# Feed-forward in two passes over its weights, half of its tokens normed inside the second, and modulation chunks moved into local attention

## The chip, the cores and the metric

One core of one Trainium2 chip runs the whole program. The metric is the device time of one execution in microseconds. A core has PE (TensorE: matmuls and transposes, results in PSUM), DVE (VectorE), ACT (ScalarE), POOL (GpSimd) and SP, whose queue issues most of the loads. Each engine works through its own list of instructions in order and waits on semaphores for the others.

## The reference

Two layers over 1024 latent tokens and 256 context tokens, 1024 wide, in fp32. Each layer mixes tokens with three kinds of attention and then runs a feed-forward part. A modulation (six vectors of 1024 per stream and layer, from one product with `w_ada`) shifts, scales and gates.

```python
m_lat = jnp.split((silu_c @ w_ada[layer] + b_ada[layer])[:, None, :], 6, axis=-1)
...
y_lat = jnp.concatenate([gla_lat, diff_lat, swa_lat], axis=-1) @ w_out[layer]
h_lat_mid = post_norm(h_lat, y_lat, m_lat[2], ln_g[layer, 0], ln_b[layer, 0])
h_lat_next = swiglu_sublayer(h_lat_mid, m_lat[3], m_lat[4], m_lat[5], w_ffn_gate[layer],
                             w_ffn_up[layer], w_ffn_down[layer], ln_g[layer, 1], ln_b[layer, 1])

def modulate(x, shift, scale):
    return (_ln_plain(x) * (1.0 + scale.astype(F32)) + shift.astype(F32)).astype(x.dtype)

def post_norm(h, y, gate, g, b):
    return layer_norm(DN_ALPHA * h + gate * y, g, b)

def swiglu_sublayer(h, shift, scale, gate, w_g, w_u, w_d, g, b):
    u = modulate(h, shift, scale)
    f = (jax.nn.silu(u @ w_g) * (u @ w_u)) @ w_d
    return post_norm(h, f, gate, g, b)
```

The context stream does the same in layer 0 with its own modulation; in layer 1 only the latent tokens go through the feed-forward. The hidden width is 2816 = 22 tiles of 128.

## The kernel before

The program is a row of stages, one after the other, each with its own buffers: modulation (the first six chunks), input norm, input projection, gated linear attention, differential attention, local (sliding window) attention, attention norm (output projection included), feed-forward, feed-forward norm; then layer 1 from its input projection on. Every stage ends with all engines done.

fp32 products are made of three matmuls: each operand is split into a high part and the rest (`hi`, `lo`), and `product` (L122 to L127) issues hi*hi, hi*lo, lo*hi.

**Feed-forward (`swiglu`, from L1965).** The 22 hidden tiles are taken as 11 groups of two. A group has six weight blocks of 128x1024 (512 KB), j = 0 to 5: gate and up of the first hidden tile, gate and up of the second, and the two down blocks. SP loads a block into `raw` (three buffers), ACT copies the high part (L2032), POOL subtracts to get the low part (L2061). The tokens are taken in `CHUNKS`: 512 and 512 latent tokens and 256 context tokens in layer 0, the first two in layer 1. For each of the two hidden tiles PE makes gate, then up, for all chunks; ACT takes silu of gate (L2040), DVE multiplies it with up (L2125), POOL splits the product into `hhi` and `hlo` (L2067, L2069). Then PE makes the down product per token tile and half, into `ffn_acc`, and DVE adds it to `Y` in SBUF (L2130), which POOL has set to zero at the start (L2057). PE waits before a tile's down product for the hidden part of the tile's chunk:

```python
                pe.wait_ge(w_ready, g * 6 + 6)
                for n, tt in enumerate(order):
                    pe.wait_ge(hid_ready, g * 2 * NC + NC + chunk_of[tt] + 1)
```

Groups 1 to 9 are a hardware loop, groups 0 and 10 are written out. ACT may overwrite a high part once its last reader is done (`release`).

**Norm of tiles (`norm_tiles`, from L216).** One function for three kinds (input, attention, ffn). Per tile of 128 tokens, for kind ffn: SP loads the residual `h_mid`; DVE multiplies `Y` by the gate (L447), adds the residual (L450), takes statistics (L424, L426); ACT takes the root (L495), DVE the reciprocal and the negated mean (L432, L434), ACT normalizes (L499), POOL multiplies by `ln_g` (L543), DVE adds `ln_b` (L456) and SP stores. In layer 0 a second normalization follows, for the next layer's input: statistics, root, normalize into `x`, eight transposes on PE (L406), eight modulating instructions on ACT (L511), high part on DVE (L469), low part on POOL (L548). The steps of neighbouring tiles are staggered by hand. In layer 0 this stage also makes eight chunks of 512 of layer 1's modulation: 2 MB of `w_ada` per chunk (L342), a product (L398), the bias (L478).

**Local attention (`sliding_window_attention`, from L1370).** Per tile of 128 queries and per key group: scores on PE, shift and maximum on DVE (L1604), exponential on ACT (L1542), scaling on POOL (L1465), transposes (L1504), product with V (L1516). The order is written out by a list of slots. SP loads keys, then the queries of two tiles, then each further tile's queries when the scores of the tile two before are made (L1453).

## Time and profile before

| | us |
|---|---|
| median of 3 runs (4255.87 to 4266.93) | 4262.75 |
| profiled execution, its own time | 4264.5 |
| its span, first to last instruction | 4262.2 |
| PE busy (of the span) | 3553.8 (83%) |
| DVE, ACT, POOL busy | 1611.0, 1299.4, 1434.5 |
| mean granted clock of PE | 0.91 |

A busy PE is one with a matmul under way; matmuls overlap, so the distance between starts is what one costs in a stream. The span is a row of stages with all engines handed over between them, so a stage can be read by itself. The granted clock is 1.00 at 2.4 GHz and 0.50 at 1.2 GHz; means over a stretch lie between.

### The profile page before, as it was taken

Reading aid. Unit: us, or ns where it says so; the run is one execution under the profiler, and the core shown is the slowest. Engines: PE = TensorE matmul, PEld = TensorE weight load, DVE = VectorE, ACT = ScalarE, POOL = GpSimd, SP = SyncE. Lnnn points to the kernel's source line nnn. Section 1 sums busy time; section 2 is a strip of 40 time slices with the busy share of each in tenths; the row PEclk is TensorE's granted clock in tenths of the full one; section 3 lists DMA queues with packets and bytes.
Section 4 is the critical chain, followed back from the end, with each engine's and each line's share of the span. In section 5 each row is a group of like instructions: output and inputs, shape, how many; then the busy total and the mean of one; then the engine's idle time right before and its main releaser. Section 6 shows DMA issues by size and latency. Waiting matters only on the chain. (4 is left out here: it accounts for less than half of the span.)

```text
span 4262.2 us, 52025 instructions
## 1 busy us (share of the span) xinstructions
PE 3553.8 (83%) x19550; PEld 2828.6 (66%) x19550; DVE 1611.0 (38%) x2555; ACT 1299.4 (30%) x2242; POOL 1434.5 (34%) x951
## 2 busy tenths in 40 slices
PE   6799596878686999999995599596966969999991
PEld 2488386555475888888881387385654758888881
DVE  2104553756472221121126404555845621222215
ACT  2211274765442011101103311375844321111111
POOL 1211242763344223323322311244923433333331
PEclk8899697788898999999997799698988979999996
DMA  8423312113331111111105323312033311111112
GB/s 287 151 86 116 100 26 64 30 37 84 102 105 58 40 40 39 34 34 44 39 15 202 132 90 111 95 31 71 15 88 90 99 59 50 49 49 49 43 36 93
DMA packets 151200, 318.19 MB, mean 75 GB/s; under 512 B 12105, under 2 KB 72489, under 8 KB 151057
## 3 DMA queue, kind: packets, MB, share of 16 engines
q1 hardware_dynamic: 128304, 260.20, 19.6%
q10 hardware_dynamic: 19072, 44.60, 2.8%
q0 software_dynamic: 3680, 11.47, 1.0%
q8 instruction: 91, 1.49, 0.1%
q14 instruction: 53, 0.43, 0.0%
HBM read 250.20 MB, written 66.03 MB: 74 GB/s over the span
## 5 line engine op out<-in xcount | busy, mean ns | idle before, releaser
L2061 POOL TENSOR_TENSOR ffn_wlo<-ffn_raw,ffn_whi 128x1024 fp32r<-128x1024 f32 x132 | 314.6, 2390 | 800.3 <-ACT ffn_whi L2032 800.3
L2125 DVE TENSOR_TENSOR ffn_hid<-ffn_up,ffn_silu 128x512 f32<-128x512 f32 (+1 forms) x110 | 70.2, 638 | 1049.0 <-PE ffn_up L127 1022.9
L2032 ACT CAST ffn_whi<-ffn_raw 128x1024 fp32r<-128x1024 f32 x132 | 136.4, 1048 | 945.1 <-PE ffn_acc L127 467.4
L2130 DVE TENSOR_TENSOR y<-ffn_acc,y 128x512 f32<-128x512 f32 x396 | 273.8, 691 | 266.8 <-PE ffn_acc L127 266.8
L125 PE MATMUL ffn_gate<-second_uhi,ffn_whi 128*128 128x512 f32 (+1 forms) x880 | 325.9, 370 | 37.3 <-POOL ffn_wlo L2061 37.3
L126 PE MATMUL ffn_gate<-second_ulo,ffn_whi 128*128 128x512 f32 (+1 forms) x880 | 325.3, 370 | 0.0
L127 PE MATMUL ffn_gate<-second_uhi,ffn_wlo 128*128 128x512 f32 (+1 forms) x880 | 325.1, 369 | 0.0
L126 PE MATMUL ffn_up<-second_ulo,ffn_whi 128*128 128x512 f32 (+1 forms) x880 | 323.9, 368 | 0.0
L125 PE MATMUL ffn_up<-second_uhi,ffn_whi 128*128 128x512 f32 (+1 forms) x880 | 323.8, 368 | 0.0
L127 PE MATMUL ffn_up<-second_uhi,ffn_wlo 128*128 128x512 f32 (+1 forms) x880 | 323.7, 368 | 0.0
L125 PE MATMUL ffn_acc<-ffn_whi,ffn_hhi 128*128 128x512 f32 x792 | 308.2, 389 | 0.0
L126 PE MATMUL ffn_acc<-ffn_wlo,ffn_hhi 128*128 128x512 f32 x792 | 308.2, 389 | 0.0
L127 PE MATMUL ffn_acc<-ffn_whi,ffn_hlo 128*128 128x512 f32 x792 | 308.1, 389 | 0.0
L637 POOL TENSOR_TENSOR in_wlo<-in_raw,in_whi 128x1024 fp32r<-128x1024 f32 x42 | 100.2, 2387 | 453.3 <-ACT in_whi L661 453.3
L1920 DVE TENSOR_SCALAR_CACHE_REDUCE diff_scores<-diff_scores 128x1280 f32<-128x1280 f32 (+1 forms) x144 | 196.7, 1383 | 66.5 <-PE diff_scores L1774 65.2
L125 PEld LDWEIGHTS ffn_gate<-second_uhi,ffn_whi 128*128 128x128 f32 x880 | 167.0, 190 | 66.3 <-POOL ffn_wlo L2061 38.1
L1844 ACT ACTIVATE diff_e<-diff_scores,diff_negmax 128x1280 f32<-128x1280 f32 (+1 forms) x144 | 178.2, 1238 | 66.8 <-DVE diff_scores L1920 65.8
L2040 ACT ACTIVATE ffn_silu<-ffn_gate 128x512 f32<-128x512 f32 (+1 forms) x110 | 61.1, 556 | 448.5 <-PE ffn_gate L127 448.5
L125 PE MATMUL in_acc<-first_uhi,in_whi 128*128 128x512 f32 (+1 forms) x504 | 179.5, 356 | 20.7 <-POOL in_wlo L637 20.7
L1898 POOL TENSOR_TENSOR diff_w<-diff_w,diff_e 128x1280 f32<-128x1280 f32 (+1 forms) x72 | 191.9, 2666 | 6.0
L126 PEld LDWEIGHTS ffn_gate<-second_ulo,ffn_whi 128*128 128x128 f32 x880 | 167.0, 190 | 28.2
L127 PEld LDWEIGHTS ffn_gate<-second_uhi,ffn_wlo 128*128 128x128 f32 x880 | 166.8, 190 | 28.0
(270 smaller groups left out, 8157.8 us busy)
## 6 DMA issues: line engine op xcount, KB each, us to landing
ffn_raw<-w_ffn_dram SPq DMA_DIRECT2D x132, 512.0 KB, 3.6
in_raw<-w_in_dram SPq DMA_DIRECT2D x42, 512.0 KB, 3.5
norm_input_ada_w<-w_ada_dram SPq DMA_DIRECT2D x10, 2048.0 KB, 9.2
norm_ffn_ada_w<-w_ada_dram SPq DMA_DIRECT2D x8, 2048.0 KB, 8.0
proj_scratch<-in_stage ACTq DMA_DIRECT2D x20, 640.0 KB, 2.9
ada_w<-w_ada_dram SPq DMA_DIRECT2D x6, 2048.0 KB
gla_kq<-proj_scratch SPq DMA_DIRECT2D x32, 320.0 KB
swa_qhl<-heads_scratch SPq DMA_DIRECT2D x36, 256.0 KB
```

Source lines behind the costliest of these rows:

```text
L125: pe.matmul(out, st_hi, mv_hi, start=start, stop=False)
L126: pe.matmul(out, st_hi, mv_lo, start=False, stop=False)
L127: return pe.matmul(out, st_lo, mv_hi, start=False, stop=stop)
L637: pool.tensor_tensor(wlo[:, s, :, :], raw[:, s, :].rearrange("p (k n) -> p k n", k=KT), whi[:, s, :, :].bitcast(F32), ALU.subtract).then_i ...
L1844: act.activation(E[:, r % 4, c, 0:keys], SC[:, c, 0:keys], ACT.Exp, bias=ng[:, c:c + 1], scale=-1.0, accum_out=den[:, c, tile_of(i, r), r ...
L1898: pool.tensor_tensor(w, w, E[:, u % 4, 0, 0:keys], ALU.add).then_inc(w_done, 1)
L1920: dve.tensor_scalar(SC[:, c, 0:keys], SC[:, c, 0:keys], -scale, 3e38, ALU.mult, ALU.min, accum_out=ng[:, c:c + 1]).then_inc(neg_done, 1)
L2032: act.copy(whi[:, j % 3, :], raw[:, j % 3, :]).then_inc(w_hi, 1)
L2040: act.activation(sg[:, c, 0:tn], GT[:, c, 0:tn], ACT.Silu).then_inc(silu_done, 1)
L2061: pool.tensor_tensor(wlo[:, j % 3, :], raw[:, j % 3, :], whi[:, j % 3, :].bitcast(F32), ALU.subtract).then_inc(w_ready, 1)
L2125: dve.tensor_tensor(hf[:, c, 0:tn], UP[:, c, 0:tn], sg[:, c, 0:tn], ALU.mult).then_inc(mul_done, 1)
L2130: dve.tensor_tensor(Y[:, tt, cols], ACC[:, half, :], Y[:, tt, cols], ALU.add).then_inc(y_added, 1)
```

## The change

Three parts.

1. `swiglu` goes over the weights twice. Pass 0 takes the first 512 latent tokens and, in layer 0, the 256 context tokens; pass 1 the other 512 latent tokens. All is written out, with no hardware loop. `raw`, and the banks of gate and up, have two buffers instead of three; silu's result is multiplied in place. The first group of a pass copies into `Y`, so nothing is set to zero.
2. In pass 1 the tiles of pass 0 are normed, one tile in each of the groups 1, 2, 4, 5, 7, 8 (layer 0) or 1, 2, 4, 5 (layer 1), with all the steps of the ffn norm, in layer 0 the transposes and the modulation too. `norm_tiles` for kind ffn is left with the last four tiles.
3. The ffn norm of layer 0 makes no modulation chunks. Local attention of layer 1 makes them, one per query tile.

```diff
-        chunked = modulated and not attn
+        chunked = kind == "input"
@@ sliding_window_attention
+            chunks = [(1, c) for c in range(4, ADA_CHUNKS)]
+            shares = [1] * len(tiles)
...
+                if b == 1:
+                    for n in range(min(AR, len(chunks))):
+                        load_chunk(n)
+                if b >= 2:
+                    for n in chunks_at(b - 2):
+                        if n + AR < len(chunks):
+                            load_chunk(n + AR)
...
+            def modulation_chunk(b, n):
+                pe.wait_ge(w_in[n % AR], 80 * (n // AR + 1))
...
+                for kt in range(KT):
+                    for j in range(4):
+                        mm = pe.matmul(O[32 * j:32 * j + 32, b % 2, k * P:(k + 1) * P], cs[:, kt, :], W[:, n % AR, kt, j * P:(j + 1) * P],
+                                       start=(kt == 0), stop=(kt == KT - 1))
+                mm.then_inc(product_done, 1)
@@ swiglu
+        passes = [CHUNKS[0:1] if last else [CHUNKS[0], CHUNKS[2]], [CHUNKS[1]]]
+        group_of = [1 + 3 * k // 2 for k in range(NT)]
...  SP
+            for p in range(2):
+                for g in range(G):
+                    if p == 0 and g == 1:
+                        load_residual(0)
+                    for j in range(6):
+                        load_weight(p, g, j)
+                        if j == 3 and p == 1 and g - 1 in group_of:
+                            k = group_of.index(g - 1)
+                            store(k)
+                            if k + 1 < NT:
+                                load_residual(k + 1)
...  ACT
+                    if k is not None:
+                        normalize(k, 0, Y[:, normed_tiles[k], :])
+                    silu(p, g, 0)
+                    split(p, g, 3)
+                    split(p, g, 4)
+                    silu(p, g, 1)
+                    split(p, g, 5)
+                    if k is not None and not last:
+                        if k == 0:
+                            act.wait_ge(one_plus, 1)
+                        normalize(k, 1, x[:, :])
+                        modulate(k)
+                    if following(p, g)[0] < 2:
+                        for j in range(3):
+                            split(*following(p, g), j)
...  PE
+                    pe.wait_ge(w_ready, weight(p, g, 5) + 1)
+                    for n, (c, tt, at) in enumerate(tiles_of(p)):
+                        pe.wait_ge(hid_ready, unit(p, g, 1, c) + 1)
+                        if n == 2 and norm_tile(p, g) is not None and not last:
+                            turn(norm_tile(p, g))
...  DVE
+                    if not last and norm_tile(p, g - 1) is not None:
+                        high_part(norm_tile(p, g - 1))
+                    if k is not None:
+                        residual(k)
+                    multiply(p, g, 0)
+                    if k is not None:
+                        shifted(k)
+                    multiply(p, g, 1)
@@ build
-                    swiglu(nc, t, res, layer, LAT_CHUNKS if last else CHUNKS)
-                    norm_tiles(nc, t, res, "ffn", layer, tiles, last)
+                    swiglu(nc, t, res, layer, last)
+                    norm_tiles(nc, t, res, "ffn", layer, everything[(N_CTX + BANK) // P:], last)
```

`residual(k)` on DVE is the product with the gate, the wait for the residual load, the sum and the statistics up to the negated mean; `shifted(k)` is the addition of `ln_b` and, in layer 0, the second statistics.

The lists of instructions show it at three places. POOL in the feed-forward of layer 0, first a group before (`wlo` low part of a weight, `hhi` and `hlo` parts of a chunk's hidden values):

```order
L2061 TENSOR_TENSOR ffn_wlo<-ffn_raw,ffn_whi 128x1024 x4
L2067 CAST ffn_hhi<-ffn_hid 128x512
L2069 TENSOR_TENSOR ffn_hlo<-ffn_hid,ffn_hhi 128x512
L2067 CAST ffn_hhi<-ffn_hid 128x512
L2069 TENSOR_TENSOR ffn_hlo<-ffn_hid,ffn_hhi 128x512
L2067 CAST ffn_hhi<-ffn_hid 128x256
L2069 TENSOR_TENSOR ffn_hlo<-ffn_hid,ffn_hhi 128x256
L2061 TENSOR_TENSOR ffn_wlo<-ffn_raw,ffn_whi 128x1024 x2
```

and now, group 2 of pass 1, with the low part of the tile of group 1 (`second_ulo`) and the scaling of its own (`y<-y,ffn_lng`):

```order
L2239 TENSOR_TENSOR ffn_wlo<-ffn_raw,ffn_whi 128x1024 x4
L2258 TENSOR_TENSOR second_ulo<-ffn_x,second_uhi 128x8x128
L2253 TENSOR_TENSOR y<-y,ffn_lng 128x1024
L2245 CAST ffn_hhi<-ffn_silu 128x512
L2247 TENSOR_TENSOR ffn_hlo<-ffn_silu,ffn_hhi 128x512
L2239 TENSOR_TENSOR ffn_wlo<-ffn_raw,ffn_whi 128x1024 x2
L2245 CAST ffn_hhi<-ffn_silu 128x512
L2247 TENSOR_TENSOR ffn_hlo<-ffn_silu,ffn_hhi 128x512
L2239 TENSOR_TENSOR ffn_wlo<-ffn_raw,ffn_whi 128x1024 x4
```

One chunk instead of three per hidden tile stands between the weights, and two instructions of the norms come behind weight 3, ahead of the hidden parts.

ACT in the same stage, before:

```order
L2032 CAST ffn_whi<-ffn_raw 128x1024 x3
L2040 ACT_TABLE_LOAD
L2040 ACTIVATE ffn_silu<-ffn_gate 128x512 x2
L2040 ACTIVATE ffn_silu<-ffn_gate 128x256
L2032 CAST ffn_whi<-ffn_raw 128x1024 x2
L2040 ACTIVATE ffn_silu<-ffn_gate 128x512 x2
L2040 ACTIVATE ffn_silu<-ffn_gate 128x256
L2032 CAST ffn_whi<-ffn_raw 128x1024 x4
```

and in group 1 of pass 1:

```order
L2191 ACT_TABLE_LOAD
L2191 ACTIVATE ffn_sd<-ffn_mv,ffn_eps 128x1
L2195 ACTIVATE y<-y,ffn_nmu,ffn_rstd 128x1024
L2187 ACT_TABLE_LOAD
L2187 ACTIVATE ffn_silu<-ffn_gate 128x512
L2179 CAST ffn_whi<-ffn_raw 128x1024 x2
L2187 ACTIVATE ffn_silu<-ffn_gate 128x512
L2179 CAST ffn_whi<-ffn_raw 128x1024
L2191 ACT_TABLE_LOAD
L2191 ACTIVATE ffn_sd<-ffn_mv,ffn_eps 128x1
L2195 ACTIVATE ffn_x<-y,ffn_nmu,ffn_rstd 128x1024
```

The root and the normalization of the tile (L2191, L2195) now stand ahead of the first silu, with a table load on either side.

SP in local attention of layer 1, before (`khh` and `kll` keys, `qhl` queries):

```order
L1447 DMA swa_khh<-heads_scratch 64x2x1408
L1448 DMA swa_kll<-heads_scratch 64x2x1408
L1447 DMA swa_khh<-heads_scratch 64x2x1408
L1448 DMA swa_kll<-heads_scratch 64x2x1408
L1453 DMA swa_qhl<-heads_scratch 64x8x128 x16
```

and now, from the queries of the first two tiles on:

```order
L1486 DMA swa_qhl<-heads_scratch 64x8x128 x4
L1476 DMA swa_ada_w<-w_ada_dram 128x8x512
L1479 DMA swa_ada_b<-b_ada_dram 2x128 x4
L1476 DMA swa_ada_w<-w_ada_dram 128x8x512
L1479 DMA swa_ada_b<-b_ada_dram 2x128 x4
L1476 DMA swa_ada_w<-w_ada_dram 128x8x512
L1479 DMA swa_ada_b<-b_ada_dram 2x128 x4
L1476 DMA swa_ada_w<-w_ada_dram 128x8x512
L1479 DMA swa_ada_b<-b_ada_dram 2x128 x4
L1486 DMA swa_qhl<-heads_scratch 64x8x128 x2
L1476 DMA swa_ada_w<-w_ada_dram 128x8x512
```

Four loads of `w_ada` (2 MB each) now lie between the queries of the second tile and those of the third.

## Rows read from the trace of the kernel before

**Rows 1.** Busy time by stage: feed-forward and norm of layer 0, then of layer 1.

```profile
core 0: us, PE busy (x) PEld busy (x) DVE busy (x) ACT busy (x) POOL busy (x), PEclk, DMA share, GB/s
1327.60:2247.40 919.80, 907.36 (x4488) 771.91 (x4488) 191.86 (x286) 101.96 (x133) 273.40 (x199) 0.99 0.12 38
2247.40:2405.90 158.50, 78.46 (x208) 22.37 (x208) 112.27 (x149) 60.69 (x121) 53.52 (x29) 0.77 0.53 186
3441.50:4175.00 733.50, 721.02 (x3168) 596.43 (x3168) 152.09 (x220) 93.52 (x111) 248.43 (x156) 0.99 0.15 47
4175.00:4262.20 87.20, 0.00 (x0) 0.00 (x0) 48.51 (x64) 13.56 (x17) 20.43 (x12) 0.52 0.33 114
```


**Rows 2.** Timeline, a group of layer 1: start us, us, engine, line; PE, DVE, POOL.

```profile
3759.67 0.39 PE L127 MATMUL ffn_up<-second_uhi,ffn_wlo 128*128 128x512 f32 x1
3759.90 0.39 PE L125 MATMUL ffn_acc<-ffn_whi,ffn_hhi 128*128 128x512 f32 x1
...
3760.16 0.69 DVE L2125 TENSOR_TENSOR ffn_hid<-ffn_up,ffn_silu 128x512 f32<-128x512 f32 x1 [4.75 <-PE ffn_up L127]
...
3761.01 0.61 POOL L2067 CAST ffn_hhi<-ffn_hid 128x512 fp32r<-128x512 f32 x1 [3.47 <-DVE ffn_hid L2125]
3761.71 1.29 POOL L2069 TENSOR_TENSOR ffn_hlo<-ffn_hid,ffn_hhi 128x512 fp32r<-128x512 f32 x1
```


**Rows 3.** Timeline of DVE: residual products of both feed-forward norms.

```profile
2265.93 1.22 DVE L447 TENSOR_TENSOR norm_ffn_h<-y,norm_ffn_gate 128x1024 f32<-128x1024 f32 x1
...
2296.95 1.23 DVE L447 TENSOR_TENSOR norm_ffn_h<-y,norm_ffn_gate 128x1024 f32<-128x1024 f32 x1 [1.38 <-ACT norm_ffn_x L499]
...
2372.49 1.98 DVE L447 TENSOR_TENSOR norm_ffn_h<-y,norm_ffn_gate 128x1024 f32<-128x1024 f32 x1 [0.75 <-ACT norm_ffn_x L499]
...
4184.34 1.22 DVE L447 TENSOR_TENSOR norm_ffn_h<-y,norm_ffn_gate 128x1024 f32<-128x1024 f32 x1 [10.12 <-DMA norm_ffn_lnb<-ln_b_dram]
...
4210.59 1.82 DVE L447 TENSOR_TENSOR norm_ffn_h<-y,norm_ffn_gate 128x1024 f32<-128x1024 f32 x1 [2.95 <-DMA out_dram<-norm_ffn_h]
...
4246.92 2.21 DVE L447 TENSOR_TENSOR norm_ffn_h<-y,norm_ffn_gate 128x1024 f32<-128x1024 f32 x1 [2.56 <-DMA out_dram<-norm_ffn_h]
```


**Rows 4.** Timeline, start of the feed-forward stage of layer 0: ACT, POOL.

```profile
1331.20 1.04 ACT L2032 CAST ffn_whi<-ffn_raw 128x1024 fp32r<-128x1024 f32 x1 [8.48 <-DMA ffn_raw<-w_ffn_dram]
...
1327.57 8.63 POOL L2057 MEMSET y<- 128x10240 f32 x1 [1.70 <-POOLq L213]
1336.16 7.00 POOL L2061 TENSOR_TENSOR ffn_wlo<-ffn_raw,ffn_whi 128x1024 fp32r<-128x1024 f32 x3
```


**Rows 5.** Timeline of PE in the attention norm, and the windows behind it.

```profile
1211.29 0.50 PE L125 MATMUL norm_attention_y<-norm_attention_wohi,norm_attention_mhi 128*128 128x512 f32 x1 [2.26 <-POOL norm_attention_mlo L539]
...
1212.10:1215.50 3.40, 3.40 (x10) 2.66 (x9) 3.19 (x8) 0.41 (x2) 0.00 (x0) 0.51 0.00 0
1215.50:1218.90 3.40, 3.40 (x16) 2.83 (x15) 3.26 (x4) 1.42 (x2) 2.19 (x1) 0.99 0.87 252
```


**Rows 6.** Timeline, steps of a norm: ACT in layer 1, DVE and ACT in layer 0.

```profile
4188.58 1.28 ACT L495 ACT_TABLE_LOAD   x1 [46.15 <-DVE norm_ffn_mv L426]
...
4190.60 1.24 ACT L499 ACTIVATE norm_ffn_h<-norm_ffn_h,norm_ffn_nmu,norm_ffn_rstd 128x1024 f32<-128x1024 f32 x1 [0.43 <-DVE norm_ffn_nmu L434]
...
2293.24 2.33 DVE L434 SCALAR_TENSOR_TENSOR norm_ffn_nmu<-norm_ffn_mv,norm_ffn_rstd 128x1 f32<-128x1 f32 x1
...
1319.83 2.90 ACT L511 ACTIVATE norm_attention_x<-norm_attention_tr,norm_attention_shift,norm_attention_scale 128x128 f32<-128x128 f32 x8 [2.06 <-PE norm_attention_tr L406]
```


**Rows 7.** DMA issues: tokens loaded in the norm (KB each, us to landing).

```profile
norm_ffn_hres<-h_mid_scratch SPq DMA_DIRECT2D x18, 512.0 KB, 4.4
```


**Rows 8.** Local attention of layer 1; a chunk in the first stage; a modulation load.

```profile
3244.00:3264.00 20.00, 19.10 (x113) 11.31 (x110) 12.59 (x32) 10.72 (x27) 7.77 (x10) 1.00 0.06 14
...
28.47 3.20 PE L184 MATMUL ada_acc<-ada_w,silu_c 128*2 128x128 f32 x64 [2.12 <-DMA ada_b<-b_ada_dram]
...
norm_ffn_ada_w<-w_ada_dram SPq DMA_DIRECT2D x8, 2048.0 KB, 8.0
```

More of the change, by code:

```diff
@@ L1414, in sliding_window_attention, with chunks_at, chunk_of @@
         heads = t["heads"]
+        if layer == 0:
+            chunks, shares = [], [0] * len(tiles)
+        else:
+            chunks = [(1, c) for c in range(4, ADA_CHUNKS)]
+            shares = [1] * len(tiles)
+        def chunks_at(b):
+            first = sum(shares[:b])
+            return range(first, first + shares[b])
+        def chunk_of(m, c):
+            b, k = m // 2, c // 2
+            return sum(shares[:b]) + k if m % 2 == 0 and 0 <= m < NG and k < shares[b] else None
         def by_act(x):
@@ L1522, in _ @@
                     score(n, j)
+                if c % 2 == 0 and chunk_of(m, c) is not None:
+                    modulation_chunk(m // 2, chunk_of(m, c))
                 if c < turns_of(m):
@@ L1583, in _ @@
                     store((n - LAG - 1) // 2)
+                _, _, m, c = slots[max(s - 2, 0)]
+                if s >= 2 and c % 2 == 0 and chunk_of(m, c) is not None:
+                    store_chunk(chunk_of(m, c))
+            for s in range(AR):
+                act.wait_ge(row_out[s], 64 * len(chunks[s::AR]))
             for s in range(2):
@@ new lines, in swiglu, with stream, columns, tiles_of @@
+        block = ctx.enter_context(nc.Block())
+        const_loads = 16 * ((0 if last else 4) + 2)
+        def stream(k):
+            return 0 if normed_tiles[k] < CTX_TILES else 1
+        def columns(p, c):
+            first = sum(tn for _, tn in passes[p][:c])
+            return slice(first, first + passes[p][c][1])
+        def tiles_of(p):
+            return [(c, t0 // P + a, columns(p, c).start + a * P) for c, (t0, tn) in enumerate(passes[p]) for a in range(tn // P)]
+        def unit(p, g, f, c):
+            return sum(2 * G * len(passes[q]) for q in range(p)) + (2 * g + f) * len(passes[p]) + c
@@ new lines, in last_unit, with y_count, y_group, weight @@
+        def last_unit(p, g, f):
+            return unit(p, g, f, len(passes[p]) - 1)
+        def y_count(p, g, n, half):
+            return sum(2 * G * len(tiles_of(q)) for q in range(p)) + 2 * (g * len(tiles_of(p)) + n) + half + 1
+        def y_group(p, g):
+            return y_count(p, g, len(tiles_of(p)) - 1, 1)
+        def weight(p, g, j):
+            return (p * G + g) * 6 + j
+        def following(p, g):
+            return (p, g + 1) if g + 1 < G else (p + 1, 0)
+        def norm_tile(p, g):
+            return group_of.index(g) if p == 1 and g in group_of else None
@@ new lines, in load_residual, with store @@
+            def load_residual(k):
+                if k:
+                    sp.wait_ge(summed, k)
+                tt = normed_tiles[k]
+                if k == 0 or stream(k) != stream(k - 1):
+                    sp.dma_start(gate[:, :], t["mod"][layer, 1 - stream(k):2 - stream(k), 5 * D:6 * D].to_broadcast([P, D])).then_inc(gate_in, 16)
+                sp.dma_start(hres[:, :], t["h_mid"][tt * P:(tt + 1) * P, :]).then_inc(h_in, 16)
+            def store(k):
+                tt = normed_tiles[k]
+                sp.wait_ge(h_done, k + 1)
+                rows = t["out"][(tt - CTX_TILES) * P:(tt - CTX_TILES + 1) * P, :] if last else t["h_next"][tt * P:(tt + 1) * P, :]
+                sp.dma_start(rows, Y[:, tt, :]).then_inc(h_out, 16)
@@ new lines, in residual @@
+            def residual(k):
+                y = Y[:, normed_tiles[k], :]
+                dve.wait_ge(gate_in, 16 * len({stream(i) for i in range(k + 1)}))
+                dve.wait_ge(y_added, y_group(0, G - 1))
+                dve.tensor_tensor(y, y, gate[:, :], ALU.mult).then_inc(gated, 1)
+                dve.wait_ge(gated, k + 1)
+                dve.wait_ge(h_in, 16 * (k + 1))
+                dve.scalar_tensor_tensor(y, hres[:, :], ALPHA, y, ALU.mult, ALU.add).then_inc(summed, 1)
+                dve.wait_ge(summed, k + 1)
+                statistics(k, 0)
```

368 lines of the change are left out of this document (243 added, 125 removed).

## Prediction

> **What bounds the kernel now.** I read the stage table first, then the pieces of single stages. The feed-forward stages take 919.8 and 733.5 us, 39% of the span, and PE is busy in 907.4 and 721.0 of them at a granted clock of 0.99 [rows 1]: they are PE's stream of matmuls and nothing else. One 512-column matmul follows the other every 0.227 us (3759.67 to 3759.90) [rows 2]. The norms behind them are the opposite: 158.5 us with 78.5 of PE and 87.2 us with none [rows 1], chains from one small instruction to the next. The change takes tiles out of those chains and puts them beside the matmuls, and pays with a second pass over the weights. So the question is what the matmul stream loses.
>
> **Norm stages.** Ten tiles become four in layer 0, eight become four in layer 1. Layer 0: the first residual product starts at 2265.93, the fourth at 2296.95, the tenth at 2372.49 [rows 3]. With four tiles the last one starts 31.0 us behind the first instead of 106.6, so 75.5 us go. The stage's head was 18.5 us (2247.4 to 2265.9) with a 2 MB modulation load ahead of it; layer 1's head without one was 9.3 (4175.0 to 4184.3) [rows 1, 3]. The new head has two loads of constants more than that, so I take 11.5 and a gain of 7. Layer 1: the fourth product (4210.59) starts 26.25 us behind the first, the eighth 62.6. 36.3 us go [rows 3]. Together **-118.8 us**. The first feed-forward matmul no longer waits for the 8.63 us memset of y: with the casts at 1331.20 + 1.04 the first low part could run from 1332.3 instead of 1336.16 [rows 4]; 3.8 us in each layer, **-7.6**. The six constant loads now issued there by POOL fit before 1332.
>
> **The bare second pass.** Matmuls keep their number: every chunk of tokens still meets every weight once. The weight preparation doubles, 132 more splits on POOL, three of which took 7.00 us [rows 4]. A group of the second pass has 96 gate and up matmuls and 48 of the down product, 144 x 0.227 = 32.7 us; POOL needs 6 x 2.33 + 2 x 1.98 = 18.0 of it (3761.01 to 3763.0 is a hidden part [rows 2]), the loads 6 x 0.5 MB. Capacity is there, at no cost. The order is the trouble. The down product of a group needs the hidden part of its last chunk of tokens. Now PE runs up of chunk 0, then up of the next chunk, which hides the way of chunk 0 through DVE (product), POOL (high part) and POOL (low part). With one chunk alone nothing stands between. The way is measured in the group shown: PE stops issuing up at 3759.90, the DVE product starts at 3760.16, the low part ends at 3761.71 + 1.29 = 3763.0, and PE would go on at 3763.1 [rows 2]. That is 3.2 us without a matmul, in 11 groups of layer 0 and 22 of layer 1 (there the first pass too has one chunk): 33 x 3.2 = **+105.6**. In layer 0's first pass the 256-column chunk (24 matmuls at about 0.125, 3.0 us) hides all but 0.2: **+2**. Bounds: 2.9 to 3.5 per group.
>
> **The clock.** A pause has a second price. At 1211.29 PE resumed after 2.26 us of idle; from 1212.1 to 1215.5 the granted clock is 0.51 (the level of 1.2 GHz), and then 0.99 again (2.4 GHz); ten matmuls went in 3.4 us where the next stretch has sixteen [rows 5]. Lost: 6 matmuls, 1.4 us, up to 1.7 where the half-rate stretch is full. Not every pause of that size did it, but most did. The new pause is longer, 2.95 us by the modelled ends. I take 1.6 us in three of four pauses: 33 x 1.2 = **+40**; bounds 0 and 56.
>
> **The normed tiles.** Six tiles in layer 0 (groups 1, 2, 4, 5, 7, 8 of pass 2), four in layer 1 (1, 2, 4, 5). All times from the group's first gate matmul; up of the second half is wanted at 16.3, the down product can start at 25.0. *First tile of a pair:* from the first product to the end of the normalize it takes 4184.34 to 4191.84, 7.5 us, the table load among it [rows 3, 6]. It starts at 0.95 and is held about 2.4 by POOL's two weight splits (a one-column DVE instruction, 0.16 elsewhere, took 2.33 beside a POOL one [rows 6]): 10.9. Another table load (1.28) and silu (0.6) on ACT: 12.8. Only then comes ACT's split of weight 3 and POOL's, 16.3: just in time. Behind it POOL has the scaling 2.4, hidden 1.9, two splits 4.8: 25.4; DVE, in the second statistics until then, gives its product at 26.4, the hidden part is there at 28.5. +3.5. Then 8 transposes, 2.0 (ACT waits 2.06 for them in the row), and ACT prepares the next group's first weight only after the 2.90 us modulation [rows 6], 1.3 late: 6.6. *Second tile of a pair:* its residual load is issued only behind this group's fourth weight and the store of the tile before, at about 4.8; 512 KB take 4.4 [rows 7] and have two such in front, so it lands near 10.6. DVE stands in front of that wait with its product behind it, ACT behind DVE: weight 3 is ready at 21.1 (PE idle 4.8), and along the same chain the hidden part at 35.3, 10.3 late; with transposes and the late weight 13.5. Layer 0: 3 x 6.6 + 3 x 13.5 = 60. Layer 1 has no second statistics, no transposes: 2.4 and 8.5, 2 x 2.4 + 2 x 8.5 = 22. Sum **+82**; bounds: 12 (the transposes alone) and 110.
> The Trainium skill, GPSIMD Engine Reference, section Specifications, says that POOL shares its SBUF interface with those DVE instructions that have two SBUF inputs; the row of 2.33 us agrees. Without such holding the first tile of a pair would cost some 2.4 us less.
>
> **Modulation chunks in local attention of layer 1.** Eight chunks. PE is busy 19.1 of 20 us there [rows 8], so its added work is exposed: a chunk of 64 matmul halves took 3.20 us in the first stage (2.8 to 3.6) [rows 8]; 8 x 3.2 = 25.6. DVE's row and POOL's zeroing are hidden (vT is loaded 12 us before the first score). ACT issues 32 stores; I add 4: **+30**. What could be late is the query load of the third tile: it now stands in SP's queue behind four 2 MB loads of 8.0 us [rows 8]. They start when the first queries are in, near 3140, and end near 3170; the tile is wanted at about 3172. Nothing taken, up to 29 us if wrong. Low end 15, high end 59. In layer 0 the chunk list is empty.
>
> **Sum.** The profiled execution took 4264.5 us (span 4262.2). -118.8 - 7.6 + 105.6 + 2 + 40 + 82 + 30 = +133; 4397.7. That execution is 1.75 above the median of the three runs (4262.75), so I say **4396 us**.
>
> **Rivals.**
> 1. *Everything but the matmul stream's own pause is absorbed* (ends on the other side, faster): the normed tiles fit in the idle of DVE, ACT and POOL, the clock stays, local attention takes the chunks in its gaps. Then -118.8 - 7.6 + 107.6 = -18.8: 4244. It decides if all costs of the second pass and of the chunks stay under 126.4 / 33 = 3.8 us per single-chunk group; the pause alone is 3.2. For it: 18 of 33 us busy on POOL. Against: the in-order queues above, and PE at 19.1 of 20 in local attention. 5%.
> 2. *The clock stays at its full level*, the rest as forecast: 4356. For it: the matmuls around the pause are dense. Against: the fall at 1212 behind a shorter pause. 25%. The Trainium skill, TensorE: Matmul & The Clock Gate, section "Why this matters for your kernels", advises against pauses only where they are about this long or longer, which would give this result; [rows 5] speak against it.
> 3. *The normed tiles cost only their transposes* (a load that comes sooner, no holding): 4396 - 70 = 4326. 12%.
> 4. *The queries wait behind the modulation weights* in SP's queue: +29, 4425. 13%.
> 5. My forecast, 45%.
>
> **How the numbers follow.** 0.3% (13 us) is about what a measurement of this kernel can tell from no change. Not slower needs rival 1 or rivals 2 and 3 at once with cheap chunks (4396 - 40 - 70 - 15 = 4271): together 7%, of which 3% is faster and 4% within 0.3%. Slower by more: 93%. The range goes from rival 3 to the forecast with the upper clock bound and dearer tiles (4396 + 16 + 28): 4325 to 4440; it holds rivals 2, 3 and 4 and leaves out 1.
>
> **What would show it.** In each single-chunk group PE idle of about 3 us in front of the down product, released by POOL's low part; the group 36 us instead of 32.7 and up to 50 in groups 2, 5 and 8; half-clock stretches of 3.4 us behind the pauses and a mean clock of the second passes near 0.95; silu late behind DVE's wait for the residual load in groups 2, 5, 8; norm stages near 76 and 51 us; local attention near 194. Wrong if PE has no idle before the down product, if the clock is 1.00 through the passes, or if groups with and without a normed tile are equally long.

## The result and the profile after

The changed kernel takes 4382.8 us in the median of 4 runs (4373.4 to 4385.5), the kernel before 4259.3 in 4 runs beside it (4254.8 to 4266.9). The ratio is 1.0285, 95% interval 1.0265 to 1.0304: 2.9% slower. The forecast was 4396, between 4325 and 4440. The profiled execution of the change took 4385.5 us (span 4383.7).

Busy time by stage, in the order of [rows 1] with local attention of layer 1 in the middle (columns as there):

```profile
1327.10:2348.20 1021.10, 946.67 (x4536) 794.45 (x4536) 261.62 (x371) 227.00 (x289) 463.87 (x284) 0.96 0.24 77
2348.20:2423.10 74.90, 7.87 (x32) 6.27 (x32) 42.76 (x57) 24.83 (x49) 23.07 (x14) 0.50 0.24 77
3130.20:3316.80 186.60, 146.46 (x1259) 99.11 (x1259) 93.78 (x233) 81.69 (x188) 52.93 (x70) 0.90 0.53 150
3480.00:4335.20 855.20, 766.65 (x3168) 622.77 (x3168) 179.12 (x252) 177.34 (x193) 413.08 (x227) 0.94 0.27 88
4335.20:4383.70 48.50, 0.00 (x0) 0.00 (x0) 23.36 (x32) 7.42 (x9) 11.94 (x8) 0.53 0.32 119
```

Against the kernel before: feed-forward of layer 0 +101.3 us, its norm -83.6, local attention of layer 1 +23.0, feed-forward of layer 1 +121.7, its norm -38.7. That is +123.7; all other stages together are 2 us shorter, and the span grew by 121.5. In layer 1 PE has the same 3168 matmuls as before, yet 45.6 us more of busy time (766.7 against 721.0) and 76 us more without any. Both are losses: most of the added busy time is matmuls that take longer where the granted clock is lower (0.94 in the mean against 0.99).

A group is called single-chunk when its pass has one chunk of 512 tokens, and bare when no tile is normed in it as well. One bare group of layer 1 (3565.4 to 3602.8) from the timeline, around the end of its last up product (start, us, engine, line, operation; in brackets the idle before and who ended it). Compare [rows 2], where the matmul at 3759.90 follows the last up matmul at once:

```profile
3586.97 0.39 PE L127 MATMUL ffn_up<-second_uhi,ffn_wlo 128*128 128x512 f32 x1
...
3587.47 0.69 DVE L2360 TENSOR_TENSOR ffn_silu<-ffn_up,ffn_silu 128x512 f32<-128x512 f32 x1 [10.19 <-PE ffn_up L127]
3588.23 0.61 POOL L2245 CAST ffn_hhi<-ffn_silu 128x512 fp32r<-128x512 f32 x1 [2.26 <-DVE ffn_silu L2360]
3588.92 1.26 POOL L2247 TENSOR_TENSOR ffn_hlo<-ffn_silu,ffn_hhi 128x512 fp32r<-128x512 f32 x1
...
3590.28 0.47 PE L125 MATMUL ffn_acc<-ffn_whi,ffn_hhi 128*128 128x512 f32 x1 [2.92 <-issue]
...
3591.54 0.63 PE L126 MATMUL ffn_acc<-ffn_wlo,ffn_hhi 128*128 128x512 f32 x1
```

PE stops, DVE multiplies, POOL makes the high and the low part, which ends at 3588.92 + 1.26 = 3590.18, and 0.1 us later PE goes on. Then the matmuls take 0.63 us instead of 0.39. The windows of that group, of the two stretches behind its pause, and of the one bare group that kept its clock:

```profile
3565.40:3602.80 37.40, 34.48 (x145) 28.06 (x145) 6.91 (x10) 7.28 (x8) 17.98 (x10) 0.95 0.26 85
...
3590.90:3594.30 3.40, 3.40 (x10) 2.62 (x9) 0.69 (x1) 0.00 (x0) 1.61 (x1) 0.51 0.17 39
3594.30:3597.70 3.40, 3.40 (x16) 2.78 (x16) 1.44 (x3) 0.00 (x0) 0.00 (x0) 0.99 0.28 116
3864.90:3900.70 35.80, 32.88 (x145) 26.92 (x145) 6.92 (x10) 7.28 (x8) 18.02 (x10) 1.00 0.29 88
```

Of the 33 single-chunk groups 23 are bare. 20 of these take 37.4 to 37.6 us and have a 3.4 us stretch at 1.2 GHz behind the pause, ten matmuls where sixteen fit; one has none and takes 35.8. The two left (38.9 us, behind a group with a normed tile, and 39.0, the first of layer 1) have a mean clock of 0.91 and 0.92 and more time at the half clock. So a pause of 2.9 us costs 1.6 us more by the clock.

The ten groups with a normed tile are longer. The second one of layer 1 (3977.8 to 4023.4, 45.6 us), DVE, ACT, PE and SP:

```profile
3978.62 1.22 DVE L2334 TENSOR_TENSOR y<-y,ffn_mod_gate 128x1024 f32<-128x1024 f32 x1
3989.03 1.23 DVE L2337 SCALAR_TENSOR_TENSOR y<-ffn_hres,y 128x1024 f32<-128x1024 f32 x1 [9.20 <-DMA ffn_hres<-h_mid_scratch]
...
3991.86 0.30 ACT L2191 ACTIVATE ffn_sd<-ffn_mv,ffn_eps 128x1 f32<-128x1 f32 x1 [10.54 <-DVE ffn_mv L2324]
3992.58 1.25 ACT L2195 ACTIVATE y<-y,ffn_nmu,ffn_rstd 128x1024 f32<-128x1024 f32 x1 [0.43 <-DVE ffn_nmu L2328]
3993.85 1.28 ACT L2187 ACT_TABLE_LOAD   x1
3995.14 0.60 ACT L2187 ACTIVATE ffn_silu<-ffn_gate 128x512 f32<-128x512 f32 x1
3995.64 1.98 ACT L2179 CAST ffn_whi<-ffn_raw 128x1024 fp32r<-128x1024 f32 x2
...
3999.15 0.79 PE L125 MATMUL ffn_up<-second_uhi,ffn_whi 128*128 128x512 f32 x1 [4.85 <-POOL ffn_wlo L2239]
...
3982.96 0.43 SPq L2144 DMA_DIRECT2D ffn_hres<-h_mid_scratch  x1
```

SP issues the residual load at 3982.96, it is there at 3989.03, and the whole row behind it (root, normalize, table load, silu, cast of weight 3, POOL's part) ends with PE idle for 4.85 us in the middle of the group.

The residual products of the two feed-forward norms, first and last of the four ([rows 3] show ten and eight):

```profile
2359.69 1.22 DVE L447 TENSOR_TENSOR norm_ffn_h<-y,norm_ffn_gate 128x1024 f32<-128x1024 f32 x1
...
2390.71 1.23 DVE L447 TENSOR_TENSOR norm_ffn_h<-y,norm_ffn_gate 128x1024 f32<-128x1024 f32 x1 [1.38 <-ACT norm_ffn_x L499]
...
4344.44 1.23 DVE L447 TENSOR_TENSOR norm_ffn_h<-y,norm_ffn_gate 128x1024 f32<-128x1024 f32 x1 [10.16 <-DMA norm_ffn_lnb<-ln_b_dram]
...
4368.29 2.34 DVE L447 TENSOR_TENSOR norm_ffn_h<-y,norm_ffn_gate 128x1024 f32<-128x1024 f32 x1 [2.43 <-DMA out_dram<-norm_ffn_h]
```

The groups of instructions on the page hold a trap:

```profile
L125 PE MATMUL ffn_acc<-ffn_whi,ffn_hhi 128*128 128x512 f32 x792 | 336.6, 425 | 117.0 <-issue 113.2
```

The idle before the down product, 117 us, is put down to "issue", time in which PE waited for nothing that the profile shows. The changed kernel is written out group after group, so fetching code is a ready story. The timeline above says otherwise (PE resumes 0.1 us behind POOL's low part, each time), but that is a reading. The first experiments were made to tell the two apart.

### The profile page after: what moved, and what is told of

Read it like the earlier page. It is cut to its first block and busy times, and to the rows that moved or that the text cites. A ratio compares the mean times of both kernels' runs of the same rounds, so it can differ in the third digit from the quotient of the medians.

```text
span 4383.7 us, 51652 instructions
## 1 busy us (share of the span) xinstructions
PE 3589.8 (82%) x19934; PEld 2878.4 (66%) x19934; DVE 1613.7 (37%) x2556; ACT 1466.7 (33%) x2400; POOL 1753.4 (40%) x1094
## 5 line engine op out<-in xcount | busy, mean ns | idle before, releaser
L2239 POOL TENSOR_TENSOR ffn_wlo<-ffn_raw,ffn_whi 128x1024 fp32r<-128x1024 f32 x264 | 638.0, 2424 | 820.6 <-ACT ffn_whi L2179 820.5
L2179 ACT CAST ffn_whi<-ffn_raw 128x1024 fp32r<-128x1024 f32 x264 | 272.4, 1050 | 969.9 <-PE ffn_acc L127 540.6
L125 PE MATMUL ffn_acc<-ffn_whi,ffn_hhi 128*128 128x512 f32 x792 | 336.6, 425 | 117.0 <-issue 113.2
L2385 DVE TENSOR_TENSOR y<-ffn_acc,y 128x512 f32<-128x512 f32 x360 | 249.0, 692 | 408.1 <-PE ffn_acc L127 408.1
L2360 DVE TENSOR_TENSOR ffn_silu<-ffn_up,ffn_silu 128x512 f32<-128x512 f32 x110 | 70.1, 638 | 876.0 <-PE ffn_up L127 859.9
L126 PE MATMUL ffn_acc<-ffn_wlo,ffn_hhi 128*128 128x512 f32 x792 | 330.7, 418 | 0.0
L127 PE MATMUL ffn_acc<-ffn_whi,ffn_hlo 128*128 128x512 f32 x792 | 330.0, 417 | 0.0
L125 PEld LDWEIGHTS ffn_acc<-ffn_whi,ffn_hhi 128*128 128x128 f32 x792 | 162.3, 205 | 166.4 <-issue 131.9
L125 PEld LDWEIGHTS ffn_up<-second_uhi,ffn_whi 128*128 128x128 f32 x880 | 168.1, 191 | 50.6 <-POOL ffn_wlo L2239 22.2
L1513 POOL TENSOR_SCALAR swa_p<-swa_p,swa_rden 128x640 f32<-128x640 f32 (+1 forms) x144 | 107.6, 768 | 228.1 <-DVE swa_rden L1698 228.1
```

The costliest lines, as they stand in the source:

```text
L125: pe.matmul(out, st_hi, mv_hi, start=start, stop=False)
L126: pe.matmul(out, st_hi, mv_lo, start=False, stop=False)
L127: return pe.matmul(out, st_lo, mv_hi, start=False, stop=stop)
L1513: pool.tensor_scalar(pr[:, m % RING, j, 0:keys], pr[:, m % RING, j, 0:keys], rden[:, m % RING, j:j + 1], 1.0, ALU.mult, ALU.mult).then_inc ...
L2179: act.copy(whi[:, w % 3, :], raw[:, w % 2, :]).then_inc(w_hi, 1)
L2239: pool.tensor_tensor(wlo[:, w % 3, :], raw[:, w % 2, :], whi[:, w % 3, :].bitcast(F32), ALU.subtract).then_inc(w_ready, 1)
```

## The experiments

My theory: the second pass loses by order, not by capacity. The down product needs the hidden part of its only chunk; the clock falls behind the pause; and in groups with a normed tile other work stands in order behind that tile's chain. Times are medians, each compared with runs of the kernel before on the same chip.

### Halves of the last up product

```diff
+  if which == 1 and alone(p, g, f):            # the last up product of a single-chunk group
+      for q in range(2):                       # columns 0:256, 256:512, each in a bank of its own
+          ...
+          mm.then_inc(done if q else half_up, 1)
...
+  if n < 2 and alone(p, g, 1):
+      pe.wait_ge(half_ready, alone_count(p, g))
+  else:
       pe.wait_ge(hid_ready, unit(p, g, 1, c) + 1)
```

DVE and POOL work on halves likewise. Expected:

> The change, with the last up product of every single-chunk group made in two halves of 256 columns (each in its own PSUM bank), so that DVE and POOL prepare the first half's hidden part while PE makes the second half; down-product tiles 0 and 1 wait only for the first half. Computes the same. Theory (the pause is one of order: the hidden part of the only chunk is on the path, and the clock falls behind it): the idle of 2.9 us before the down product goes in the bare groups, at the price of 48 matmuls of 0.125 us for 24 of 0.227 (+0.55 us), and the half-clock stretches behind it go too (-1.6 us in 32 groups): 33 x (2.9 - 0.55) + 51 = 129 us less than the change, about 4255, between 4235 and 4275; a bare group takes 33.5 us. Rival A (the time of the second pass is instruction issue or code loading, because everything is written out, as the idle that the page puts down to issue suggests): 24 matmuls more per group make it no faster, 4383 to 4400. Rival B (POOL or the weight loads have no room): the pause moves to the next gate or up product, under 30 us gained.

Measured: 4273.2 us (10 runs), ratio to before 1.0025 [1.0016, 1.0035]; 110 us less than the change. The windows of a bare group, then of the first two groups with a normed tile in layer 1:

```profile
3561.00:3594.00 33.00, 33.00 (x170) 28.30 (x169) 7.07 (x11) 7.30 (x8) 18.33 (x12) 1.00 0.30 96
3857.80:3895.70 37.90, 34.85 (x170) 29.50 (x169) 14.86 (x19) 11.30 (x12) 22.86 (x13) 0.95 0.26 84
3895.70:3940.90 45.20, 37.01 (x170) 31.29 (x169) 12.79 (x19) 11.18 (x12) 21.83 (x13) 0.89 0.28 94
```

In the bare group PE is busy 33.0 of 33.0 us at the full clock, with 24 matmuls more, and POOL is busy 18.3 us of it. The pause is gone in all 23 bare groups, 37.4 to 33.0, which makes 101 us. Fetching and capacity (rivals A and B) are out, and the step from three buffers to two, which this kernel has too, costs the bare groups nothing. The 18 us that lack to the theory's 4255 are in the other ten: they gained only 0.9 us each, and still wait for about 3 us or more in front of the down product. They take 102 us more than ten bare ones. That is the rest to be explained.

### Matmuls without use in the pause

```diff
     pe.wait_ge(w_ready, weight(p, g, 5) + 1)
+    if len(passes[p]) == 1:
+        ...
+        for k in range(12):
+            pe.matmul(TR[:, 0:4, :]..., whi[:, 1, ...], uhi[:, k % KT, t0:t0 + tn], start=True, stop=True)
```

> The change, with 12 matmuls without use (512 columns, into the transposes' PSUM banks) in front of the down product of every single-chunk group, where PE has a pause of 2.9 us. They fill about 12 x 0.227 = 2.7 us of it and make it no shorter. Theory (the clock term is a price of its own, 1.6 us in each of 32 groups): the bare groups keep the granted clock at 1.0 and take 35.8 us instead of 37.4; the ten groups with a normed tile, whose pauses are longer, keep some of theirs: 35 to 50 us less than the change, 4333 to 4350. Rival (the slower matmuls behind the pause are something else than the idle before them, or the clock falls anyway): 4383, and half-clock stretches remain.

Measured: 4347.5 us, ratio 1.0197 [1.0180, 1.0214]; 35.3 us less than the change, by doing more. The window of a bare group:

```profile
3586.30:3622.20 35.90, 35.72 (x158) 29.23 (x158) 6.92 (x10) 7.32 (x8) 18.06 (x10) 1.00 0.27 88
```

The bare groups take 35.8 to 36.0 us at clock 1.00 (the first of layer 1 38.8). 22 bare groups times 1.6 are 35.2. The clock's price is its own term and stands behind the idle, as the theory had it. The ten others hardly changed.

### The loops of before written out

`for g in range(1, G - 1)` in place of the hardware loop, on every engine of the feed-forward.

> The kernel before, with the hardware loops of its feed-forward written out, group after group, nothing else. Theory: writing out costs nothing, since PE's matmuls of 0.227 us leave the fetching of instructions far behind: within 5 us of the before kernel, 4254 to 4264. Rival (code loading: the changed kernel's idle that the page puts down to issue, 113 us, is the price of the written-out loop): slower by 20 us up to 113.

Measured: 4261.0 us (10 runs), ratio 1.0001 [0.9991, 1.0010]. Its two feed-forward stages:

```profile
1321.40:2241.70 920.30, 907.82 (x4488) 772.26 (x4488) 191.99 (x286) 102.23 (x133) 273.63 (x199) 0.99 0.12 38
3440.40:4173.60 733.20, 720.69 (x3168) 596.40 (x3168) 152.19 (x220) 93.72 (x111) 248.79 (x156) 0.99 0.15 48
```

and, on its page, the group of instructions that had 117.0 us of idle in the change:

```profile
L125 PE MATMUL ffn_acc<-ffn_whi,ffn_hhi 128*128 128x512 f32 x792 | 308.2, 389 | 0.0
```

The same 792 instructions, written out, without any idle: written-out code costs nothing here, and "issue" was POOL's hidden part.

### The modulation chunks alone

The kernel before with the changed local attention, and without chunks in the norm behind the feed-forward.

> Only the last part of the change: the eight modulation chunks in local attention of layer 1 instead of in the norm behind layer 0's feed-forward; the feed-forward and its ten or eight normed tiles are those of before. Theory: local attention of layer 1 +23 us and of layer 0 +3 as in the trace of the change, the norm behind the first feed-forward 8 us shorter (no 2 MB load ahead of its first residual): 4259 + 26 - 8 = 4277, between 4270 and 4285. Rival (the chunks did cost something between the tiles of the norm, and moving them pays for itself): 4259 or less. Rival (part of the 23 us comes from what the new feed-forward leaves behind, such as the state of the queues): local attention grows by less than 15 us.

Measured: 4282.5 us (5 runs, 4276.5 to 4293.5), ratio 1.0049 [1.0032, 1.0066]; 21.8 us slower than before. Local attention of layer 1 takes 187.6 us, within 1 us of the change's 186.6, so nothing of its 23 us comes from the new feed-forward. The norm behind the feed-forward of layer 0 takes 154.0 instead of 158.5: 4.5 gained, not 8. The two make 19.5 of the 21.8; the profiled execution was a long one (4291.2), so the rest cannot be placed. The windows of that norm and of local attention:

```profile
2249.40:2403.40 154.00, 19.66 (x80) 15.68 (x80) 107.24 (x141) 60.40 (x121) 53.52 (x30) 0.51 0.25 82
3118.00:3305.60 187.60, 147.54 (x1259) 99.18 (x1259) 94.00 (x233) 81.73 (x188) 52.73 (x70) 0.90 0.52 149
```

PE did 78.5 us of work in that norm before [rows 1] and does 19.7 now, for 4.5 us of time: the chunks ran there in time that was free. Moving them is a loss of its own.

### The residual loads a tile earlier

```diff
-  hres = sb(nm + "hres", [P, D])
+  hres = sb(nm + "hres", [P, 2, D])
...
   if p == 0 and g == 1:
       load_residual(0)
+      load_residual(1)
...
-  if k + 1 < NT:
-      load_residual(k + 1)
+  if k + 2 < NT:
+      load_residual(k + 2)
```

> The change, with two buffers for the residual and two for the modulation gate, and each residual load issued a tile earlier, so that the second tile of a pair finds it landed. Theory (in the five groups with the second tile of a pair DVE stands waiting for that load, with its product, ACT's silu and split of weight 3 queued behind): their up pause (3.1 to 4.9 us) goes and part of the pause before the down product; they take what the first of a pair takes, 41.2 instead of 48.2 to 50.3 in layer 0 (three groups) and 39.8 instead of 45.6 in layer 1 (two): -24 -12 = -36, about 4347, between 4338 and 4360. Rival (the loads are not the limit, the engines' work is): under 8 us gained.

Measured: 4346.8 us, ratio 1.0197 [1.0180, 1.0214]; 36 us less than the change, the number expected. In the five groups the pause before the second up product is gone: 43.3 to 43.8 us instead of 48.2 to 50.3 in layer 0, 39.7 and 39.8 instead of 45.6 in layer 1. In layer 0 that is not the 41.2 of the theory: the pause before the down product there is still 6.0 us. So these groups gave 28 us, not 36. In the trace 8 more came from the clock: five bare groups kept its full level behind their pause, where one did in the change, and behind two pauses of layer 1 the half clock was shorter. That this made up the difference is luck.

### Silu and weight 3 ahead of the normalize

```diff
-  if k is not None:
-      normalize(k, 0, Y[:, normed_tiles[k], :])
   silu(p, g, 0)
   split(p, g, 3)
+  if k is not None:
+      normalize(k, 0, Y[:, normed_tiles[k], :])
```

> The change, with one thing moved on ACT: in a group with a normed tile silu of the first half and the split of weight 3 come before the tile's square root and normalize instead of behind them. Theory (what costs in these groups is what stands queued behind the normalize on an in-order engine): the up pause of 3.1 to 4.9 us in five groups goes although the residual load is as late as before, and POOL comes to the hidden part some 2 us earlier in the others: 5 x 6 + 5 x 2 = 40 us less than the change, about 4343, between 4330 and 4360. Rival (DVE's wait for the load holds its own product and that holds everything, in whatever order ACT works): at most 10 us gained.

Measured: 4344.5 us, ratio 1.0192 [1.0175, 1.0209]; 38 us less than the change. The pause before up is gone with the load as late as ever: it was what stands behind the wait that cost, not the wait. But in layer 1's late tiles the pause only moves in part, from 4.9 before up and 3.7 before the down product to 0 and 6.7.

### Without normed tiles in the pass

`normed_tiles = []`, and the norm stages have ten and eight tiles again.

> The change without its normed tiles: two passes over the weights, but all ten and eight tiles normed behind them as before; the modulation chunks are in local attention as in the change. Theory: the ten groups fall to 37.4 us, which takes 46 us from layer 0 and 21 from layer 1, and the norms take their 75 and 38 us back: 4383 - 67 + 113 = 4429, between 4418 and 4440; so norming inside the second pass earns some 45 us even as it stands, and the pass itself is the loss. Rival (the normed tiles cost more than they save): 4383 or less.

Measured: 4432.6 us, ratio 1.0397 [1.0379, 1.0416]; 49.7 us more than the change (46 expected). The windows of its feed-forwards:

```profile
1323.20:2294.50 971.30, 929.00 (x4488) 783.25 (x4488) 192.16 (x287) 169.00 (x199) 426.22 (x271) 0.98 0.23 73
...
3508.50:4342.00 833.50, 759.08 (x3168) 617.76 (x3168) 152.20 (x220) 161.59 (x177) 396.94 (x224) 0.95 0.26 85
```

The feed-forwards are 971.3 and 833.5 us against 1021.1 and 855.2: the normed tiles cost 50 and 22 us there and save 79 and 39 in the norm stages. Norming in the pass earns some 50 us even in its first form. The loss is the second pass itself, 51.5 us and 100.0 us over the feed-forwards of before.

### All three together, and two steps more

The halved up product, the earlier residual loads and the earlier weight 3 in one kernel, edited as above.

> The split up product, the earlier residual loads and the earlier split of weight 3 together. With the split alone (4273) a bare group takes 33.0 us and the ten groups with a normed tile 102 us more than ten bare ones. Theory: with nothing queued behind the load or the normalize these ten keep the eight transposes (1.0 us), the late first weight (0.9) and half-clock stretch behind small pauses, some 3.5 us each in layer 0 and 0.5 in layer 1: 23 instead of 102, so 4194, between 4180 and 4225: faster than before by 1 to 2%. Rival (each of the two removes the same waits, and POOL's work in these groups, about 25 of 33 us, is the limit): 4235 or more.

Measured: 4210.1 us, ratio 0.9879 [0.9863, 0.9896]: 1.2% faster than before. The theory had 4194. The ten groups take 40 us more than bare ones, not 23; each keeps 1.4 to 2.8 us before the down product. POOL in the group that begins at 3857.7, from the hidden part of the first half on:

```profile
3874.63 2.16 POOL L2271 TENSOR_TENSOR ffn_hlo<-ffn_silu,ffn_hhi 128x512 fp32r<-128x512 f32 x1
3876.74 4.72 POOL L2251 TENSOR_TENSOR ffn_wlo<-ffn_raw,ffn_whi 128x1024 fp32r<-128x1024 f32 x2
3881.41 0.40 POOL L2259 CAST ffn_hhi<-ffn_silu 128x256 fp32r<-128x256 f32 x1
3881.89 0.72 POOL L2261 TENSOR_TENSOR ffn_hlo<-ffn_silu,ffn_hhi 128x256 fp32r<-128x256 f32 x1
```

POOL works without a break through all these rows, and the down product begins at 3882.72, behind 3881.89 + 0.72 = 3882.61. In this group POOL's queue sets the end. So the next kernel takes one piece out of it: DVE scales the tile by `ln_g`, and ACT splits the next group's weight 0 ahead of `modulate`.

```diff
-  pool.tensor_tensor(Y[:, tt, :], Y[:, tt, :], lng[:, :], ALU.mult).then_inc(h_scaled, 1)
+  dve.tensor_tensor(y, y, lng[:, :], ALU.mult).then_inc(h_scaled, 1)
...
   normalize(k, 1, x[:, :])
+  split(*following(p, g), 0)
   modulate(k)
```

> The combination of before (4210) with two more moves: the scaling of a normed tile by its norm weights goes from POOL to DVE, and ACT splits the next group's first weight ahead of the modulation instead of behind it. With the combination the ten normed groups take 40 us more than ten of 33.0: each has 1.4 to 2.8 us in front of the down product while POOL still makes the split of weight 5 and the first hidden half, four of them a half-clock stretch behind it, and in layer 0 the next group begins 0.9 late. Theory (POOL's queue of 2.4 us pieces is what is left, and the scaling is one of them): the pauses of 1.4 to 2.1 us go and the half-clock stretches with them, and the 0.9: 9 x 1.7 + 4 x 1.7 + 6 x 0.9 = 27 us less, 4183, between 4175 and 4200. Rival (DVE is as late as POOL there, since the tile's second statistics stand before its product): 4205 or more.

Measured: 4187.0 us, ratio 0.9822 [0.9798, 0.9846]; 23 us less than the kernel with three edits (27 expected). The two moves were not run apart, but ACT's shows by itself: the 0.9 us before the next group's first gate product is gone behind all six normed tiles of layer 0, 5.5 us. The feed-forward stages:

```profile
1331.80:2271.30 939.50, 922.45 (x4800) 792.91 (x4800) 281.13 (x388) 235.56 (x295) 461.35 (x299) 0.99 0.26 83
3404.00:4143.20 739.20, 727.91 (x3696) 623.33 (x3696) 204.88 (x278) 178.16 (x193) 417.26 (x267) 0.99 0.32 102
```

739.2 us for layer 1 with four of its eight tiles normed inside, 5.7 us more than before without any. Over bare groups of 33.0 us its four normed ones take 1.9 us more in all; the six of layer 0 still take 15, among them 6 x 1.0 of transposes.

### The queries ahead of the weights

```diff
   if b == 1:
-      for n in range(min(AR, len(chunks))):
+      for n in range(min(2, len(chunks))):
           load_chunk(n)
-  if b >= 2:
-      ...
+  if b >= 2 and b < len(chunks):
+      load_chunk(b)
```

The rows of the change on which it rests, SP's queue and PE in local attention of layer 1:

```profile
3165.31 0.39 SPq L1476 DMA_DIRECT2D swa_ada_w<-w_ada_dram  x1
3170.89 3.04 SPq L1486 DMA_DIRECT2D swa_qhl<-heads_scratch  x2
...
3184.47 0.39 PE L1535 MATMUL swa_scores<-swa_khh,swa_qhl 128*128 128x256 f32 x1 [4.13 <-DMA swa_qhl<-heads_scratch]
```

> The kernel of 4187 us (split product, early residual, scaling on DVE), with the modulation weights of local attention loaded one per tile behind that tile's queries, two ahead of the third tile instead of four. In the trace of the change PE waits 4.1 us at 3184.5 for the queries of the third tile, which SP issues at 3170.9, behind the four weight loads. Theory (the 23 us of the chunks are 16.9 us of their own matmuls, about 1 us at the start and this wait): the wait goes, the matmuls stay; local attention of layer 1 takes 183 us instead of 187, the kernel 4183, which is within the spread of its runs: the stage in the trace decides. Rival (the wait is the loads' share of the DMA engines, not their order): the stage stays at 187 or more, with a wait of 4 us or over at the third tile or at a chunk's weights.

Measured: 4183.6 us (5 runs), ratio 0.9816 [0.9803, 0.9829]. The stage is 181.4 us instead of 187.2, and the wait at the third tile is gone:

```profile
3040.00:3221.40 181.40, 144.86 (x1259) 97.78 (x1259) 93.90 (x233) 81.90 (x188) 52.73 (x70) 0.91 0.55 154
```

The loads that stand ahead of the queries were the cause. The share of the DMA engines over the whole stage (0.55 against 0.53) hides the stretch that counts, here in the change:

```profile
3165.00:3184.50 19.50, 14.57 (x146) 10.70 (x145) 12.12 (x32) 10.33 (x27) 6.94 (x9) 1.00 1.08 345
```

The DMA engines are busy throughout, and the queries issued at 3170.9 are used only at 3184.5. The edit has them issued sooner and with two 2 MB loads ahead of them instead of four. Which of the two helped, the place in SP's queue or the fewer bytes under way, is not separated. Nor is it traced why the stage gained 5.8 us where the wait was 4.1. The 3.3 us between the two medians are within their spread; the stage in the trace is what shows it. This is the best kernel of the study, 1.8% faster than before.

## Why the prediction was right

Each term of the sum against what the trace shows, in us:

| term | forecast | measured |
|---|---|---|
| norm stages | -118.8 | -122.3 |
| start of the feed-forwards | -7.6 | -6 |
| pause, 33 groups | +105.6 (3.2 each) | +104 (3.15 each) |
| first pass of layer 0 | +2 | +3.4 |
| clock | +40 | +51 |
| normed tiles | +82 | +69 (67 in the ten groups, 2 in those behind them) |
| modulation chunks | +30 | +23 |
| sum | +133 | +122.1 (span: +121.5) |

**The pause** stands as it was read from [rows 2]. A group of one chunk took half of 65.3 us before, 32.65, and takes 35.8 at the full clock. 2.9 us of the 3.15 are idle by the modelled ends; the rest is the overlap that a pause takes away (neighbouring matmuls are 0.39 us long and start 0.23 apart) and the slower start behind it (0.30 us from the first matmul to the second). Halving the up product removes it and writing out the loop does not make it. **The first pass** lost 0.3 us per group instead of 0.2. That the doubled weight preparation costs nothing was right too: the first-pass groups of layer 0 are 50.0 us, all but the very first, and the halved bare ones are 33.0 with 18.3 of POOL.

**The clock** term was mis-sized in its share. "1.6 us in three of four pauses" was right in the 1.6; but 22 of 23 bare pauses had it. In the ten other groups it is part of their excess. In the table all 33 groups but one stand with 1.6. [Rows 5] had shown it once behind 2.26 us; "most did" was said of pauses shorter than 2.9 us. Rival 2 is out, and the kernel with filled pauses shows what it would have been worth in the bare groups, 35 us.
The Trainium skill, TensorE: Matmul & The Clock Gate, section "Why this matters for your kernels", advises against idle gaps between bursts of matmuls that are about as long as these or longer. The prediction drew rival 2 from it, that a pause just short of that keeps the clock. Behind pauses of 2.9 us the half clock followed in 22 of 23 bare groups, so the advice has to be read to include them.

**The normed tiles.** In layer 1 the chain was read right: 2.4 and 8.5 forecast, 2.3 and 8.2 measured (39.7 and 45.6 over 37.4). In layer 0 it was 6.6 and 13.5, measured 3.2 to 4.9 and 10.8 to 12.9. Two steps failed there. "8 transposes, 2.0": ACT's wait of 2.06 us in [rows 6] is not PE's time, which is 1.0 for eight; and the delay of the hidden part, "+3.5", is 1.2 to 2.0 (pauses of 4.1 to 4.9 us against 2.9). (The terms as written, 3.5 + 2.0 + 1.3 and 10.3 + 2.0 + 1.3, add to 6.8 and 13.6 and not to 6.6 and 13.5; that moves the whole sum by 1 us.) The residual load was forecast to land 10.6 us into the group and was used at 9.6 to 10.4 in layer 0 and 11.2 in layer 1. So rival 3, the transposes alone, is out: 69 us against 12.

**The norm stages.** Layer 0's new head was put at 11.5 us and is 2359.69 - 2348.20 = 11.5; the last product stands 31.0 behind the first, as forecast. Layer 1's is 23.9 behind, not 26.25, since the last two come sooner.

**The modulation chunks** came out near the forecast because its errors cancel in part. "A chunk of 64 matmul halves took 3.20 us in the first stage": at what clock was that? The window of that very row in the kernel before:

```profile
28.47:31.67 3.20, 3.20 (x64) 2.12 (x64) 0.00 (x0) 0.00 (x0) 0.00 (x0) 0.59 1.05 410
```

and the chunks in the local attention of the change, by its groups of instructions:

```profile
L1579 PE MATMUL swa_o_acc<-swa_ada_w,swa_ada_c 128*32 128x128 f32 x512 | 16.9, 288 | 0.0
```

The granted clock was 0.59 there and is near full here: 16.9 / 8 = 2.1 us a chunk, 16.9 instead of 25.6. ACT's 32 stores, "I add 4", left nothing that shows. And "nothing taken" for the queries was wrong: they cost 4.1 us, 5.8 by the experiment. Rival 4's mechanism was there, at a fifth of its 29 us, because the third tile's queries were issued at 3170.9, needed at 3180.3 and there at 3184.5. The start lost another 0.9: the first score comes 24.8 us into the stage instead of 23.9.

The closeness of the sum is partly luck too: the normed tiles and the chunks were put 20 us too high, the clock 11 us too low.

"PE idle released by POOL's low part" was right in the matter and wrong in the label: the page calls most of it issue. The group of 36, up to 50 in groups 2, 5 and 8, the half-clock stretches of 3.4 us, the mean clock (0.93 and 0.94 against 0.95), the norms of 76 and 51 (74.9 and 48.5) and local attention of 194 (186.6) came near.

## What to carry to other kernels

Where a loop over several chunks becomes a loop over one, look for the consumer that used to run behind another chunk: here the down product, whose pause of 2.9 us and the half clock behind it came in 33 groups and ate what the shorter norms saved. Halving the last piece for itself, so that the first half is prepared under the second, made the pass nearly free (33.0 us against 32.65). And when small work is put beside a full engine, what counts is not whether the helpers have time but what stands in order behind each of their waits: a silu and a cast moved ahead of a normalize, or one load issued a tile sooner, were worth 38 and 36 us (28 us of the 36 in the groups concerned). Read a duration together with the granted clock of its own window before it goes into a sum.
